# Layer two's front of the first tile and the sample, done in pieces inside layer one's last expert steps

## The chip, the cores and the metric

The kernel runs on one core of one Trainium2 chip. The metric is device microseconds of one execution. The kernel before takes 2525.78 us, the median of three runs (2523.29 to 2528.25).

## The reference, cut to what matters

One step of a two-layer encoder for 256 prompt tokens and 64 sample tokens, all in fp32. Each layer has a *mixer* half and a *PEER expert* half:

```python
h = rmsnorm(x, norm1_g);  z = h @ w_in          # xa, ga, xq, q, k, v, gates
ya = rg_lru(causal_conv(xa)) * gelu(ga)         # recurrence along the tokens
yb = pool_mixer(xq)                             # windows of 2, 4, 8, 16 tokens
yc = diff_attention(rotary(q), rotary(k), v)    # 8 heads, chunk-causal; the sample also sees its cache
x = x + (sum over branches of sigmoid(gate) * (branch @ proj)) @ w_out
h = rmsnorm(x, norm2_g);  top 16 of 16384 experts per head, 8 heads
x = x + sum(gelu(h . u[i]) * gate * v[i])       # u, v are gathered rows of 4 KB each
```

Tokens depend on each other only through the convolution, the recurrence, the pooling and the attention, and only on earlier tokens of the same stream. So the first 128 prompt tokens and the sample need nothing of the second 128 prompt tokens.

## The kernel before, in words

The 320 tokens lie in three tiles: tile 0 (prompt tokens 0 to 127), tile 1 (128 to 255, "tile two" in the texts) and tile 2 (the 64 sample tokens, held twice). Each engine has its own in-order program; they meet at counting semaphores only, so an instruction that waits holds up everything behind it on its engine.

A layer has three stages. The **front** normalises, turns h into HT, and makes the six feed-forward units of w_in (conv input, gelu gate, pooling input; `ff`, L1041 on PE), the convolution, the recurrence, the pooling, and then the eight attention heads (`head`: PE L919, ACT L1213, DVE L1475; rotary on POOL L678), ending with the heads' outputs turned into YT. In layer two its weights are loaded by SP from L527 on; the 21 parameter loads (L466) wait there for the end of layer one. The **merge** follows, and then the **expert stage**: 80 steps (`for s in range(GROUPS)`: PE L1143, ACT L1408, DVE L1856), 32 for tile 0, 16 for tile 2 and 32 for tile 1, in this order. POOL (`gathers`, L703) gathers four rows of 8 KB per token and step (1 MB each) into a ring of up to 12 buffers; a buffer is free again when PE has used it (`uv_free`). Two buffers join at picks 84 and 160 (`JOIN`, L81). The queries and the merge of tiles 1 and 2 run inside the earlier steps; in steps 41 to 72 DVE routes one of four parts of a coming unit per step (`ROUTES`, L145).

One step is a loop through three engines. DVE makes four dot products (`dots`, L1614), ACT their gelu (`weights`, L1239), DVE the routing part and then the weighing (`weigh`, L1623), ACT four diagonal matrices, and PE the matmuls that add the four rows (`experts`, L1001):

```python
                    dots(l, t, s)                    # DVE, L1861
                    ...
                        route(l, unit, [part])       # L1889
                    if s > 0:
                        weigh(l, t, g, s)            # L1891
```

On PE, tile 0's and tile 2's turns of layer two stand in step 78 (L1171), and the first feed-forward unit of their columns behind the last step (L1174).

Of the kernel before, what the change touches and what calls it, by code (L numbers as in the profile page):

```python
# [80 lines left out]
JOIN = [0] * 10 + [84, 160]  # L81
SLOT_OF, PREV, NTH = [], [], []
for _p in range(PICKS):
    _last = [max([q for q in range(_p) if SLOT_OF[q] == r], default=r - len(JOIN)) if JOIN[r] <= _p else PICKS
             for r in range(len(JOIN))]
    _r = _last.index(min(_last))
    PREV.append(max(_last[_r], -1))
    NTH.append(SLOT_OF.count(_r))
    SLOT_OF.append(_r)
RING_USES = [SLOT_OF.count(r) for r in range(len(JOIN))]  # L90
# [13 lines left out]
FF_SLOT = (0, 2, 3, 4, 1, 0)  # L104
# [29 lines left out]

def route_step(unit, part):
# [12 lines left out]
class Signal:  # L148


    def __init__(self, sem, per_layer, unit=1, start=0):
        self.sem, self.per_layer, self.unit, self.start = sem, per_layer, unit, start

    def at(self, l, n):

        return self.sem, (l * self.per_layer + n) * self.unit + self.start


def build(nc, x_prompt, x_sample, cache_v, state_conv, state_lru, state_pool,
# [3 lines left out]
          rot_table, pool_inv, layer_consts, peer_uv, gains, merge_w, out_w, query_w,  # L163
# [4 lines left out]
    with ctx:  # L168
# [45 lines left out]
        SALL12 = cut(2, 2 * PH, NK, at=0)  # L214
        SHIFT = cut(D_MODEL)
        W = sb("W", [P, SLOTS, KC, UNIT])
        W2 = [W[:, i].rearrange("p c n -> p (c n)").rearrange("p (k c n) -> p k c n", k=2, c=KC) for i in range(SLOTS)]
# [4 lines left out]
        SALL0 = cut(2 * PH, NK, at=0)  # L222
        HN0 = cut(D_MODEL)
# [28 lines left out]
        ZS = cut(2, 3 * HW)  # L252
        SUMS = [(S1, S2)[c % 2][:, c, :] for c in range(RC)]

        POOL_PARTS = ((POOL_HIST, SEQ, 0), (XQ_S + POOL_HIST, DEC_SEQ, SEQ))
# [30 lines left out]
        LCON = sb("LCON", [P, 3])  # L286
# [7 lines left out]
        PINV = sb("PINV", [P, 4, TOK])  # L294
# [48 lines left out]
        w_in_slot = [landing(f"w_in_slot{i}", SLOT_USES[i]) for i in range(SLOTS)]  # L343
        w_used = [signal(f"w_used{i}", SLOT_USES[i], start=1) for i in range(SLOTS)]
        qkv_in = [landing(f"qkv_in{i}", HEADS // 2) for i in range(2)]
        cache_in = [landing(f"cache_in{i}", 2 * HEADS // 2) for i in range(2)]
# [12 lines left out]
        ff_ps = signal("ff_ps", 6)  # L359
        ff_ev = signal("ff_ev", 12)  # L360
        xc_ready = signal("xc_ready", 1)
        bd_ps = signal("bd_ps", 2 * RC)
        sig_ev = signal("sig_ev", 2 * RC)
        decay = signal("decay", 1)
        oma = signal("oma", 1)
        root = signal("root", 1)
        ya_ready = signal("ya_ready", 1)
        d_ready = signal("d_ready", 1)
        pl_ps = signal("pl_ps", RC)
        pl_ev = signal("pl_ev", RC)  # L370
# [56 lines left out]
        uv_in = [landing(f"uv_in{i}", RING_USES[i]) for i in range(len(JOIN))]  # L427
# [38 lines left out]
        def small_loads(l):  # L466

            def row(name, n=1):
                return rows[ROW[name]:ROW[name] + n, :]
# [5 lines left out]
            def blocks(w, half):  # L475
# [12 lines left out]
                (SKR[:, :, :], peer_subkeys[l].rearrange("a k d -> k a d")),  # L488
# [19 lines left out]
        def _(sp):  # L508
# [18 lines left out]
            for l in range(DEPTH):  # L527
# [10 lines left out]
                for dst, src in loads:  # L538
                    sp.dma_start(dst, src).then_inc(small_in.sem, 16)
# [918 lines left out]
        def _(dve):  # L1458
# [242 lines left out]
            for t in SEQ_T:  # L1701
                normed(0, 0, t)
# [260 lines left out]
```

## Time and profile before

| | |
|---|---|
| time, median of three | 2525.78 us |
| the profiled execution's own time | 2523.54 us |
| its span, first to last instruction | 2521.6 us |
| mean granted TensorE clock | 0.883 |
| busy: PE, DVE, POOL, ACT | 75%, 63%, 31%, 27% |
| moved by DMA | 852 MB, mean 338 GB/s |

The span is 1.9 us shorter than the time of the same execution. Busy shares are means over stages with different limits, so the rows further down are read by stage. An fp32 matmul shows as two records. "Idle before" in square brackets is how long the engine had stood still, and what released it.

### The profile page before, as it was taken

Reading aid. Unit: us, or ns where it says so; the run is one execution under the profiler, and the core shown is the slowest. Engines: PE = TensorE matmul, PEld = TensorE weight load, DVE = VectorE, ACT = ScalarE, POOL = GpSimd, SP = SyncE. Lnnn points to the kernel's source line nnn. Section 1 sums busy time; section 2 is a strip of 40 time slices with the busy share of each in tenths; the row PEclk is TensorE's granted clock in tenths of the full one; section 3 lists DMA queues with packets and bytes.
Section 4 is the critical chain, followed back from the end, with each engine's and each line's share of the span. In section 5 each row is a group of like instructions: output and inputs, shape, how many; then the busy total and the mean of one; then the engine's idle time right before and its main releaser. Section 6 shows DMA issues by size and latency. Waiting matters only on the chain.

```text
span 2521.6 us, 31152 instructions
## 1 busy us (share of the span) xinstructions
PE 1898.0 (75%) x10740; PEld 1077.2 (43%) x10740; DVE 1588.6 (63%) x4318; ACT 677.9 (27%) x1691; POOL 780.1 (31%) x831
## 2 busy tenths in 40 slices
PE   7999988887777645555589999888777866555554
PEld 6556876654333211111165568765543432111111
DVE  3544165566788878777536431665666888777764
ACT  2423033332223222212233221333322332222121
POOL 0121022333333444344202210233334324344432
PEclk9999999999888877787899999999988887688777
DMA  6134849999999999999742357699999999999996
GB/s 217 65 130 166 316 199 417 417 412 419 419 413 369 418 421 400 421 421 421 326 155 78 126 205 270 275 417 417 404 419 420 415 370 410 403 411 421 421 421 271
DMA packets 156764, 852.11 MB, mean 338 GB/s; under 512 B 19312, under 2 KB 39280, under 8 KB 72640
## 3 DMA queue, kind: packets, MB, share of 16 engines
q0 software_dynamic: 95280, 677.24, 65.0%
q1 hardware_dynamic: 61328, 172.89, 18.7%
q8 instruction: 86, 1.41, 0.2%
q14 instruction: 70, 0.57, 0.1%
HBM read 843.35 MB, written 6.71 MB: 337 GB/s over the span
## 4 chain that ended last, share of the span: by engine, by line
DMA 30%; PE 23%; DVE 14%; issue 9%; PEld 8%; PEldq 5%; POOL 5%; DVEq 3%; ACT 2%; SPq 0%; ACTq 0%; POOLq 0%
DMA MIX_RINGS<-in_peer_uv_dram,IDX 15%; DMA WQKV_E<-in_peer_uv_dram,IDX 10%; PE ps L775 7%; PEldq L1019 5%; PEld ps L843 4%; DMA W<-in_peer_uv_dram,IDX 4%; PE ps L1049 3%; POOL MIX_RINGS L724 3%; PE ps L793 3%; DVE MIX_RINGS L1620 3%; DVEq L1464 3%; POOL W L724 2%; PE ps L781 2%; DVE W L1620 1%; PE ps L803 1%
## 5 line engine op out<-in xcount | busy, mean ns | idle before, releaser
L1017 PE MATMUL ps<-MIX_RINGS,GC 64*64 64x512 f32 x3200 | 662.0, 750 | 211.3 <-ACT GC L1248 200.0
L724 POOL DMA_INDIRECT MIX_RINGS<-in_peer_uv_dram,IDX x400 | 433.4, 1084 | 765.5 <-PEq L1019 442.0
L1017 PE MATMUL ps<-W,GC 64*64 64x512 f32 x1456 | 418.3, 776 | 297.4 <-ACT GC L1248 292.2
L1017 PEld LDWEIGHTS ps<-MIX_RINGS,GC 64*64 64x64 f32 x3200 | 158.3, 161 | 519.4 <-issue 288.5
L724 POOL DMA_INDIRECT W<-in_peer_uv_dram,IDX x182 | 196.0, 1077 | 439.5 <-PEq L1019 379.0
L1620 DVE CUSTOM_DVE_ANT_0 MIX_RINGS<-MIX_RINGS 128x1024 f32<-128x1024 f32 x224 | 269.0, 1223 | 83.3 <-DMA MIX_RINGS<-in_peer_uv_dram,IDX 78.9
L1017 PEld LDWEIGHTS ps<-W,GC 64*64 64x64 f32 x1456 | 97.7, 167 | 517.7 <-ACT GC L1248 295.7
L1248 ACT ACTIVATE GC<-twins,WV 128x64 f32<-128x64 f32 x640 | 170.3, 336 | 527.1 <-DVEq L1633 526.8
L1620 DVE CUSTOM_DVE_ANT_0 MIX_RINGS<-MIX_RINGS,WQKV_E 128x1024 f32<-128x1024 f32 x176 | 212.6, 1224 | 151.7 <-DMA MIX_RINGS<-in_peer_uv_dram,IDX 145.6
L1242 ACT ACTIVATE GV<-AV 128x4 f32<-128x4 f32 x160 | 32.9, 205 | 723.8 <-DVEq L1621 723.5
L1620 DVE CUSTOM_DVE_ANT_0 W<-W,MIX_RINGS 128x1024 f32<-128x1024 f32 x126 | 153.9, 1224 | 59.6 <-DMA W<-in_peer_uv_dram,IDX 52.2
L843 PE MATMUL ps<-HT,W 128*128 128x192 f32 x768 | 145.2, 351 | 44.0 <-issue 34.7
L775 PE MATMUL ps<-WQKV_E,HT 128*128 128x384 f32 x512 | 171.5, 489 | 0.0
L843 PEld LDWEIGHTS ps<-HT,W 128*128 128x128 f32 x768 | 138.0, 207 | 51.2 <-issue 51.1
L671 POOL TENSOR_TENSOR rot_a<-MIX_RINGS,ROTT 128x128 f32<-128x128 f32 (+1 forms) x48 | 19.9, 432 | 374.6 <-ACT MIX_RINGS L1210 374.6
L1017 PE MATMUL ps<-WQKV_E,GC 64*64 64x512 f32 x464 | 125.2, 662 | 2.2 <-ACT GC L1248 1.1
L775 PEld LDWEIGHTS ps<-WQKV_E,HT 128*128 128x128 f32 x512 | 95.0, 190 | 61.2
L906 PE MATMUL ps<-HT,W 128*128 128x256 f32 x512 | 114.3, 381 | 4.3 <-issue 4.3
L906 PEld LDWEIGHTS ps<-HT,W 128*128 128x128 f32 x512 | 96.0, 190 | 30.4 <-issue 18.0
L1620 DVE CUSTOM_DVE_ANT_0 W<-W,WQKV_E 128x1024 f32<-128x1024 f32 x56 | 68.5, 1226 | 49.7 <-DMA W<-in_peer_uv_dram,IDX 48.0
L724 POOL DMA_INDIRECT WQKV_E<-in_peer_uv_dram,IDX x58 | 64.1, 1105 | 107.2 <-PEq L1019 92.5
L1242 ACT ACT_TABLE_LOAD x72 | 92.4, 1283 | 1.3
(276 smaller groups left out, 2784.0 us busy)
## 6 DMA issues: line engine op xcount, KB each, us to landing
W<-in_merge_w_dram SPq DMA_DIRECT2D x40, 1024.0 KB, 5.0
W<-in_merge_w_dram SPq DMA_DIRECT2D x60, 512.0 KB, 14.1
WQKV_E<-in_qkv_w_dram SPq DMA_DIRECT2D x16, 1536.0 KB, 7.1
W<-in_query_w_dram SPq DMA_DIRECT2D x16, 1024.0 KB, 11.4
W<-in_w_in_dram SPq DMA_DIRECT2D x12, 1024.0 KB, 11.5
W<-in_query_w_dram SPq DMA_DIRECT2D x20, 512.0 KB, 11.4
W<-in_out_w_dram SPq DMA_DIRECT2D x8, 1024.0 KB, 13.9
MIX_RINGS<-in_peer_uv_dram,IDX POOLq DMA_INDIRECT x400, 14.6
```

The costliest lines, as they stand in the source:

```text
L724: pool.indirect_dma_start(UV[r], None, table, bass.IndirectOffsetOnAxis(IDX[:, n % DEEP, j:j + 1], 0))\
L775: i = pe.matmul(bank(n % 2, 0, 3 * HW), HT[:, c, COLS[t]], WQKV[par][:, c, :], start=c == 0, stop=c == KC - 1)
L793: i = pe.matmul(two(bank(b, 0, UNIT)), HT[:, c, 0:P], W2[b][:, :, c, :], start=c == 0, stop=c == KC - 1)
L843: m = pe.matmul(to, w[:, r, :], moving[:, r, P:TOK], start=n == 0, stop=n == len(rows) - 1)
L906: i = pe.matmul(bank(4 + 2 * slot, k * UNIT, (k + 1) * UNIT), W2[slot][:, k, c, :], HT[:, c, P:TOKD], start=c == 0, stop=c == KC - 1)
L1017: pe.matmul(ps[o:o + CHUNK, n:n + 512], w[r, :], v[r, d * 512:(d + 1) * 512], start=False, stop=False, skip_group_check=True)
L1019: pe.drain().then_inc(uv_free.sem, 2)
L1049: i = pe.matmul(bank(4 + n % 2, 0, TOK), W[:, FF_SLOT[u], c, k * P:(k + 1) * P], HT[:, c, 0:TOK], start=c == 0, stop=c == KC - 1)
L1242: act.activation(GV[:, :], AV[:, :], ACT.Gelu).then_inc(gv_ready.sem, 1)
L1248: act.activation(DG[:, p % N_DG, :], twins[:, 0:CHUNK], ACT.Copy, scale=WV[:, j:j + 1])\
L1464: dve.drain()
L1620: dve.tensor_tensor_reduce(u, u, HN[t], 1.0, 0.0, ALU.mult, ALU.add, AV[:, j:j + 1])
```

## The change

Layer two's front is split. For tile 0 and the sample (192 columns) it becomes 59 pieces, r = 0 to 58, two to each of the steps 50 to 79 of layer one (`A_SLOT` = 100). Piece 2s - 100 stands before the step's experts on PE, between gelu and diagonals on ACT, and behind the dots on DVE; piece 2s - 99 stands behind the experts on PE, behind the diagonals on ACT and behind `weigh` on DVE. Pieces 0 to 2 turn the tiles and the parameters, 3 to 14 are twelve feed-forward blocks of 128 columns, 7 to 10 the pooling, 15 to 22 the convolution and recurrence. Head h has pieces k = r - 19 - 4h: k = 0 and 1 the two halves of its qkv product, (2) the rotary on POOL, 3 the turns of q and k, 4 scores and maxima, exponentials, 5 probabilities, 6 their turns, 7 the value product and the output's squares; so k = 4 of one head shares a slot with k = 0 of the next, 5 with 1, 6 with 2, 7 with 3. Pieces 55 to 58 normalise the outputs and turn them. On DVE pieces k = 3 and 7 wait for PE's transposes and value product, and k = 5 for ACT's exponentials.

SP loads the parameters, a second, block-wise copy of the feed-forward columns (`early_w`, 512 KB a block), the qkv weights in halves of 768 KB and the caches for it, at the end of layer one's queue. POOL does head h's rotary and four stores ahead of gather 248 + 8h. The scratch for it lies in weight slots, so layer one's ring has eleven buffers from pick 84 to 180 and ten after it. The front behind layer one does tile 1 alone (128 columns): conv, pooling and recurrence start from kept states, and tile 0's keys and values are loaded back from the outputs. Also: the pooling's table of reciprocals becomes a small table of ratios, the score blocks of tiles 1 and 2 are copied by two instructions, and all three gate products stand behind the last head.

```diff
+RING = 12
+STAYS = (((0, PICKS),) * 10 + ((84, 180), (PICKS, PICKS)), ((0, PICKS),) * 10 + ((84, PICKS), (160, PICKS)))
...
+A_SLOT = 100
+A_HEADS = 19
+A_PACE = 4
...
+A_ROTARY = [4 * ((A_SLOT + A_HEADS + A_PACE * _h + 1) // 2) + 8 for _h in range(HEADS)]
...
+                    sp.wait_ge(*sso_ready.at(EARLY, 1))
+                    for u in range(3):
+                        ff_unit(u)
...
+                            sp.dma_start(KV0[:, par, 0, :], k_prompt[l, 0, 0:P, h].rearrange("p m d -> p (m d)"))\
+                                .then_inc(cache_in[par].sem, 16)
...
+                    parameters(1)
+                    for j in range(3 * RC):
+                        if j < 2:
+                            sp.wait_ge(*uv_free.at(0, 1 + max(p for p in range(PICKS) if SLOT_OF[0][p] == 10)))
+                        else:
+                            sp.wait_ge(*ff_ps.at(EARLY, j - 1))
+                        sp.dma_start(A_F[j % 2].rearrange("p c n -> p (c n)"), early_w[0, j])\
+                            .then_inc(w_in_slot[3 + j % 2].sem, 16)
...
+                            sp.wait_ge(*z_ps.at(EARLY, 3 * h + 1))
+                            early_half(h + 1, 0)
+                            sp.wait_ge(*z_ps.at(EARLY, 3 * h + 3))
+                            early_half(h + 1, 1)
...
+                pool.wait_ge(*z_ev.at(EARLY, 2 * h + 1))
+                rotate(EARLY, 2 * h, A_ZH[:, par:par + 1, :], ROTT[:, 0:1])
+                pool.wait_ge(*z_ev.at(EARLY, 2 * h + 2))
+                rotate(EARLY, 2 * h + 1, A_ZS[par].rearrange("p (t n) -> p t n", t=1), ROTT[0:DEC_SEQ, 2:3])
...
+                    if l == 0 and p in A_ROTARY:
+                        early_rotary(A_ROTARY.index(p))
...
+                    pe.wait_ge(*w_in_slot[3 + j % 2].at(0, SLOT_USES[3 + j % 2] + j // 2 + 1))
+                    if j >= 2:
+                        pe.wait_ge(*ff_ev.at(EARLY, j - 1))
+                    for c in range(KC):
+                        i = pe.matmul(bank(j % 2)[:, A_COLS], A_F[j % 2][:, c, :], HT[:, c, A_COLS],
+                                      start=c == 0, stop=c == KC - 1)
+                    i.then_inc(ff_ps.sem, 1)
...
+                for h in reversed(range(HEADS)):
+                    early_head(h, r - A_HEADS - A_PACE * h)
...
+                if k in (0, 1):
+                    pe.wait_ge(*qkv_in[k].at(EARLY, h + 1))
...
+                    w = (A_W0, A_W1)[k]
+                    for to, cols in ((bank(0, 0, 3 * HW), COLS[0]), (bank(1, 0, 3 * HW)[0:DEC_SEQ], COLS[2])):
+                        for c in range(KC // 2):
+                            i = pe.matmul(to, HT[:, k * KC // 2 + c, cols], w[:, c, :], start=k == 0 and c == 0,
+                                          stop=k == 1 and c == KC // 2 - 1, skip_group_check=True)
...
+                if k == 4:
+                    pe.wait_ge(*qt_ev.at(EARLY, h + 1))
+                    pe.wait_ge(*kt_ev.at(EARLY, h + 1))
+                    for m in range(2):
+                        pe.matmul(bank(2 + m, 0, P), A_QT[d[m], 0:P], A_KT[d[m], 0:P], start=True, stop=True,
+                                  skip_group_check=True).then_inc(s_ps.sem, 1)
...
+                if k == 6:
+                    pe.wait_ge(*p_ready.at(EARLY, 2 * h + 1))
+                    pe.transpose(bank(3, 0, P), A_PC[0], ident[:, :]).then_inc(pta_ps.sem, 1)
+                    pe.wait_ge(*p_ready.at(EARLY, 2 * h + 2))
+                    for c in range(3):
+                        i = pe.transpose(bank(2, c * CHUNK, (c + 1) * CHUNK),
+                                         A_PC[2][0:DEC_SEQ, c * P:(c + 1) * P], ident[0:DEC_SEQ, 0:DEC_SEQ])
+                    i.then_inc(ptb_ps.sem, 1)
...
+            def late_head(h):
+
+                g, par = divmod(h, 2)
+                z = ZH[par][:, 1, :]
+                pe.wait_ge(*rot_done.at(LATE_F, 2 * h + 2))
+                pe.wait_ge(*ex_done.at(LATE_F, 2 * h))
+                pe.transpose(bank(2, 0, P), z[:, 0:HW], ident[:, :]).then_inc(qt_ps.sem, 1)
+                pe.wait_ge(*pta_ev.at(LATE_F, h))
+                pe.wait_ge(*cache_in[par].at(LATE_F, 2 * g + 2))
+                pe.transpose(bank(3, 0, P), KV0[:, par, 0, :], ident[:, :])
+                pe.transpose(bank(3, P, 2 * P), z[:, HW:2 * HW], ident[:, :]).then_inc(kt_ps.sem, 1)
+                if h + 1 < HEADS:
+                    late_qkv(h + 1, range(KC // 2))
...
+                for m in range(2):
+                    d = slice(m * HD, (m + 1) * HD)
+                    pe.matmul(scores(1, m), QT[d, 0:P], KT[d, 0:2 * P], start=True, stop=True,
+                              skip_group_check=True).then_inc(s_ps.sem, 1)
+                if h + 1 < HEADS:
+                    late_qkv(h + 1, range(KC // 2, KC))
...
+                    if l == 0 and 2 * s >= A_SLOT:
+                        early(2 * s - A_SLOT)
                     experts(l, s)
+                    if l == 0 and 2 * s >= A_SLOT:
+                        early(2 * s + 1 - A_SLOT)
...
                 act.activation(GV[:, :], AV[:, :], ACT.Gelu).then_inc(gv_ready.sem, 1)
+                if l == 0 and 2 * s >= A_SLOT:
+                    early(2 * s - A_SLOT)
                 act.wait_ge(*wv_ready.at(l, s + 1))
...
+                if l == 0 and 2 * s >= A_SLOT:
+                    early(2 * s + 1 - A_SLOT)
...
+            def early_head(h, k):
...
+                if k == 4:
+                    dve.wait_ge(*s_ps.at(EARLY, 4 * h + 4))
...
+                if k == 6:
+                    dve.wait_ge(*ptb_ps.at(EARLY, h + 1))
+                    dve.tensor_copy(A_PTB, bank(2, 0, 3 * CHUNK)).then_inc(ptb_ev.sem, 1)
...
+                    if l == 0 and 2 * s >= A_SLOT:
+                        early(l, 2 * s - A_SLOT)
...
                     if s > 0:
                         weigh(l, t, g, s)
+                    if l == 0 and 2 * s >= A_SLOT:
+                        early(l, 2 * s + 1 - A_SLOT)
```

## Rows read from the trace of the kernel before

**Rows 1.** The page, the span in 40 slices: PE's and the DMA engines' line.

```profile
PE   7999988887777645555589999888777866555554
...
DMA  6134849999999999999742357699999999999996
```

**Rows 2.** Windows: late expert steps of layer one; layer two's front in three parts.

```profile
core 0: us, PE busy (x) PEld busy (x) DVE busy (x) ACT busy (x) POOL busy (x), PEclk, DMA share, GB/s
...
1062.00:1252.40 190.40, 106.64 (x624) 27.01 (x624) 126.14 (x303) 37.48 (x115) 77.61 (x69) 0.79 0.98 408
...
1257.40:1346.50 89.10, 80.33 (x346) 55.65 (x347) 44.86 (x85) 31.95 (x67) 5.59 (x11) 0.98 0.36 122
1346.50:1484.60 138.10, 133.66 (x649) 79.90 (x649) 67.34 (x253) 40.53 (x131) 35.11 (x76) 0.99 0.40 138
1484.60:1497.10 12.50, 11.76 (x57) 8.72 (x56) 5.53 (x8) 6.86 (x13) 0.00 (x0) 0.98 0.57 205
```

**Rows 3.** Timeline of ACT: the gelu of steps 49 and 79 of layer one.

```profile
954.67 0.21 ACT L1242 ACTIVATE GV<-AV 128x4 f32<-128x4 f32 x1 [0.84 <-DVEq L1621]
...
1252.16 0.20 ACT L1242 ACTIVATE GV<-AV 128x4 f32<-128x4 f32 x1
```

**Rows 4.** Timeline, layer two's front: the last experts, single pieces, the gates (start, length).

```profile
1256.67 0.60 PE L1017 MATMUL ps<-WQKV_E,GC 64*64 64x512 f32 x2
...
1266.36 3.81 PE L1029 MATMUL ps<-HT,W 128*128 128x128 f32 x32 [0.83 <-ACT HT L1200]
...
1324.85 8.23 DVE L1783 RECIPROCAL MIX_RINGS<-MIX_RINGS 128x1292 f32<-128x1292 f32 x1
...
1478.42 3.11 POOL L735 DMA_DIRECT2D out_dram<-SOT  x6 [5.20 <-DMA out_dram<-MIX_RINGS]
...
1484.56 7.17 PE L793 MATMUL ps<-W,HT 128*128 128x256 f32 x32
```

**Rows 5.** Timeline, layer two's heads: the links of one head.

```profile
1420.43 2.75 PE L775 MATMUL ps<-WQKV_E,HT 128*128 128x384 f32 x8
...
1423.11 0.93 PE L953 MATMUL ps<-MIX_RINGS 64*128 64x128 f32 x8
...
1426.01 0.47 ACT L1222 ACTIVATE MIX_RINGS<-ps,nb 128x256 f32<-128x256 f32 x1 [0.45 <-DVE nb L1493]
...
1428.04 0.17 DVE L1500 RECIPROCAL rec<-sme 128x2 f32<-128x2 f32 x1
...
1429.38 0.16 DVE L1500 RECIPROCAL rec<-sme 64x2 f32<-64x2 f32 x1
...
1433.36 0.36 DVE L1516 COPY MIX_RINGS<-ps 128x192 f32<-128x192 f32 x1 [2.68 <-PE ps L983]
```

**Rows 6.** Timeline of DVE, step 50 of layer one: first dot, routing, weighing.

```profile
957.21 1.23 DVE L1620 CUSTOM_DVE_ANT_0 MIX_RINGS<-MIX_RINGS 128x1024 f32<-128x1024 f32 x1 [0.16 <-issue]
...
962.00 0.49 DVE L1549 MAX8 MX<-WQKV_E 128x8 f32<-128x128 f32 x2
...
964.20 0.16 DVE L1628 TENSOR_TENSOR WV<-GV,GATE 128x4 f32<-128x4 f32 x1
```

**Rows 7.** Timeline, steps 68 and 69: routing, weighing and the expert matmuls behind it.

```profile
1141.98 0.17 DVE L1577 TENSOR_SCALAR CI<-BC 128x16 uint32<-128x16 uint32 x1
...
1145.83 0.16 DVE L1628 TENSOR_TENSOR WV<-GV,GATE 128x4 f32<-128x4 f32 x1
...
1150.51 1.12 PE L1017 MATMUL ps<-W,GC 64*64 64x512 f32 x2
...
1152.53 0.59 PE L1017 MATMUL ps<-W,GC 64*64 64x512 f32 x2
...
1154.07 0.16 DVE L1628 TENSOR_TENSOR WV<-GV,GATE 128x4 f32<-128x4 f32 x1
...
1156.29 2.65 PE L1017 MATMUL ps<-MIX_RINGS,GC 64*64 64x512 f32 x18
```

**Rows 8.** The page, DMA issues: 512 KB loads of merge_w on SP's queue (KB, us to landing).

```profile
W<-in_merge_w_dram SPq DMA_DIRECT2D x60, 512.0 KB, 14.1
```

More of the change, by code:

```diff
@@ L151, in __init__ @@
     def __init__(self, sem, per_layer, unit=1, start=0):
-        self.sem, self.per_layer, self.unit, self.start = sem, per_layer, unit, start
+        self.sem, self.unit, self.start = sem, unit, start
+        self.before = [sum(per_layer[:i]) for i in range(len(per_layer) + 1)] if isinstance(per_layer, tuple)\
+            else [i * per_layer for i in range(DEPTH + 2)]
     def at(self, l, n):
-        return self.sem, (l * self.per_layer + n) * self.unit + self.start
+        return self.sem, (self.before[l] + n) * self.unit + self.start
 def build(nc, x_prompt, x_sample, cache_v, state_conv, state_lru, state_pool,
@@ new lines, in late_qkv @@
+            def late_qkv(h, cs):
+                par = h % 2
+                if cs[0] == 0:
+                    pe.wait_ge(*qkv_in[par].at(LATE_F, h // 2 + 1))
+                    if h >= 2:
+                        pe.wait_ge(*z_ev.at(LATE_F, h - 1))
+                for c in cs:
+                    i = pe.matmul(bank(par, 0, 3 * HW), HT[:, c, COLS[1]], WQKV[par][:, c, :],
+                                  start=c == 0, stop=c == KC - 1)
+                if cs[-1] == KC - 1:
+                    i.then_inc(z_ps.sem, 1)
@@ new lines, in ff @@
+                        act.drain().then_inc(ff_ev.sem, 1)
+                for u in range(5):
+                    ff(u)
+                for c in range(RC):
+                    for j, (dst, row) in enumerate(((RG, "lru_ba"), (IG, "lru_bx"))):
+                        act.wait_ge(*bd_ps.at(LATE_F, 2 * c + j + 1))
+                        act.activation(dst[:, c, 0:P], bank(6 + j, 0, P), ACT.Sigmoid,
+                                       bias=PT[:, c, ROW[row]:ROW[row] + 1]).then_inc(sig_ev.sem, 1)
@@ new lines, in late_front @@
+                for h in range(HEADS):
+                    late_head(h)
+                act.wait_ge(*sso_ready.at(LATE_F, 1))
+                act.activation(rso[:, 1, :], sso[:, 1, :], ACT.Sqrt, bias=eps_c[:, :], scale=1.0 / HW)\
+                    .then_inc(sso_root.sem, 1)
+                gates(l, 0)
+                for hh in range(HEADS):
+                    act.wait_ge(*yt_ps.at(LATE_F, hh + 1))
+                    act.activation(YT[:, 2 * RC + hh, B_COLS], bank(6 + hh % 2, 0, P), ACT.Copy, scale=SUBG[:, 0:1])\
+                        .then_inc(yt_ev.sem, 1)
@@ L1325, in _ @@
                         .then_inc(yt_ev.sem, 1)
+            squares(SEQ_T)
+            turned(0, 0, SEQ_T)
+            for l in range(DEPTH):
+                if l == 0:
+                    joint_front()
+                else:
+                    late_front(l)
                 for u in range(GB):
                     if u + 1 < GB:
-                        gates(u + 1)
+                        gates(l, u + 1)
                     act.wait_ge(*mta_ps.at(l, u + 1))
@@ L1943 @@
     proj_ab = _np.concatenate([inputs["proj_a"], inputs["proj_b"]], axis=1)
+    order = [2 * RC + i for i in range(RC)] + [RC + i for i in range(RC)] + list(range(RC))
+    rows["early_w"] = blocks(inputs["w_in"][1:2, :, 0:COL_Q])[:, order]
     rows["gains"] = _np.concatenate([*(inputs[n][l:l + 1] for l in range(DEPTH) for n in ("norm1_g", "norm2_g")),
```

930 lines of the change are left out of this document (760 added, 170 removed).

## The prediction

> **What bounds the kernel now.** I read the page's slices first, then the windows by stage, then the timeline inside a stage. In the slices [rows 1] the pattern runs twice, once per layer: a front in which PE is mostly at 8 or 9 and DMA mostly at 1 to 5, then a long expert stretch in which DMA is at 9 and PE falls to 5. The windows put numbers on layer two's front and on layer one's last steps [rows 2]. In the late expert steps the DMA engines are at 0.98 and 408 GB/s, PE, on paper, 56% busy, DVE 66%. In the front behind, PE is 90% busy before the heads, 97% in them and 94% in the tail, with DMA at 0.36 to 0.57. So the front, 89.1 + 138.1 + 12.5 = 239.7 us, belongs to PE, the expert steps belong to the gathers. From the first to the second gelu of [rows 3] there are 30 steps in 297.5 us: 9.92 us each, four gathers of 1.05 MB at 422 GB/s.
>
> **The front behind: what it gives back.** It keeps 128 of 320 columns.
> Before the heads: tile two's HT is ready 9.0 us after the last expert matmul, as now (1257.3 to 1266.4 [rows 4]). Thirty-two 128-column matmuls (one unit; every fp32 matmul shows as two) take 3.81 us there, so five units take 19.1, ending at 28; the parameters are loaded beforehand, so the wait before the 320-column units goes. Then the gates' products and sigmoids (5), eight activations with a table load (4), 1 - a with its reciprocal (8.23 us for 1292 elements [rows 4], so 3.3 for 512, with two passes beside it 4.7), root, products and scans (3.3), the gelu product and the state's way through PE and DVE (3.3): 48.6 in place of 89.1, **-40.5**.
> Heads: now 17.3 each. For one tile the chain is: three transposes and half a qkv product (0.6 + 2.75 + 0.55 to start the scores) 3.9; scores to the maximum's scaling 2.1 (2.9 from 1423.11 to 1426.01, less tile one's 0.8 between); two exponentials 1.05; normalised difference 1.35 (1428.04 to 1429.38); transposes, copy, value product 1.9 (estimated as two thirds of what three tiles take): 10.3 [rows 5]. Eight, the last without a qkv half: 80.2, **-57.9**. The other qkv half (2.75) and POOL's rotary lie beside the chain. SP's key and value reloads and the 1.5 MB weights are issued a head or more ahead, POOL's store waits are bounded below.
> Tail: all three gate products now stand behind the last head (48 matmuls; 32 took 7.17 [rows 4], so 10.8), then eight small transposes and copies: 14.5, **+2**. Sum **-96**; between -78 (12 us a head, weights 5 us late) and -107 (9 us a head).
>
> **The expert steps: what it costs.** DVE runs its queue in order. One step without the pieces is, on DVE: four dots 4.8 (957.21 to 962.00 [rows 6]), one routing part (2.2 in this step [rows 6], 3.85 for the index part [rows 7]; I take 2.7 as the mean of the four), the weighing 0.3: 7.8, under the 9.9 of the gathers. What the change adds there, by rows: one head's maxima 2.1, probabilities 2.7 (twice 1.35), the KT copy and the output's copy and squares 2.0, a PTB copy 0.4, so 7.2 for two steps, which alone would still fit (22.8 us of DVE work against 25 of transfers with the new bytes).
> But the odd pieces stand right behind weigh(s) on DVE and right behind experts(s) on PE, and experts(s) itself waits for weigh(s). For k=4 (scores) and k=6 (probabilities turned) DVE asks for what PE issues in that same odd slot. So DVE stands idle while ACT builds the diagonals and PE runs the whole expert group, with the next step's dots queued behind the wait though their rows have landed. From weighing to the last expert matmul is 7.3 us in one step and 4.9 in the next [rows 7]; I take 6.3, since PE begins each burst after a pause, as in the first of them, where matmuls show 1.12 and then 0.59 us. In the k=4 slot PE also does the next head's first half *before* the scores (heads run in reverse): 16 recorded matmuls of 384 columns, twice the eight that took 2.75 us [rows 5], 5.4; scores with the cache 1.8.
> Step with k=4: 4.8 + 2.0 + 2.7 + 0.3 + 6.3 + 5.4 + 1.8 + 2.1 = 25.4. Step with k=6: 4.8 + 2.7 + 2.7 + 0.3 + 6.3 + 1.4 + 0.4 = 18.6. Eight pairs at 44.0 are 352, less 5.4 (no ninth head) and 10.8 (routing ends at step 72, four steps): 336 where 16 steps took 158.9, **+177**.
> Steps 50 to 60: the first waits for PE with the parameters, 17; step 51, 10. The twelve feed-forward blocks need 512 KB each, two a step, and each load waits for the block two before it; now such loads take 14.1 us to land in a busy stretch [rows 8]. By bytes alone a step would take (4.19 + 1.05) MB / 422 GB/s = 12.4, by landing plus some 2.9 us of matmuls (three quarters of the 3.81 of [rows 4], since a block has half the matmuls at 1.5 times the columns) 17: I take 14 for six steps, 84, nearer to the bytes since slower steps thin the gathers out. Then 12 (two taps), 12, and 19.4 (reciprocal 5.0 of 792 elements, scans). Sum 154 where 11 took 109: **+45**. Steps 77 to 79 finish the normalising: **-2**.
> Priced at nothing: ACT's pieces (3.2 us of exponentials with a table load hide behind the dots; uncovered, 3 a head); POOL's eight rotations and 32 stores ahead of the gathers (some 7 us each, behind a step pair of 44 with the ring full; in 10 us steps they would empty it); SP's 65 further loads, of which the halves are issued two steps ahead (layer two's own first loads come behind them, with all of the last steps to land); two smaller ACT copies for one per score block; the smaller pool table; ten ring slots in place of twelve from step 45 (ten sufficed for full DMA in the early slices, at most +10).
> Sum: 177 + 45 - 2 - 96 = **+124**. The profiled execution took 2523.54 us for a span of 2521.6, and the median of three is 2525.78, 2.2 above; 2523.5 + 124 gives 2647, and I say **2645**.
>
> **Rivals.** *The transfers stay the bound, and the change wins.* DMA at 0.98 in the late steps with idle PE speaks for it [rows 2]: a step then costs only its bytes, 6.3 + 12.6 + 2.1 + 0.8 = 21.8 MB at 422 GB/s, +52, net -44: **2479**. It needs the two waits of a head, 21 us together in my sum, to be under some 2 us; the net is zero at 21 - 124/8 = 5.5. Against it: the program's order, and [rows 5], where DVE's copy waits for PE in just this manner. The Trainium skill (Perfetto Trace Analysis, Identifying the Most-Contended Engine, and its Optimization Strategy) says to judge a regime by its busiest resource and to interleave regimes with different ones. By that rule this rival holds and the time is 2479. The row of this stretch agrees about which resource is busiest, but the rule does not price an in-order queue that waits in between.
> *PE stays at its lower level.* The clock granted in late steps is 0.79 [rows 2]; if the pieces run at 1.2 GHz, each head costs 1.0 more per wait, 5.4 more for the half and 1.8 for the scores, 8 x 9.2 = 74, less 5 for the last half: **2715**.
> *The front shrinks less.* POOL's wait for each store's landing (5.20 us [rows 4]) with the rotation and two issues makes about 8 us a head, under 10.3; were it 12.5, +18: **2663**.
>
> **How the numbers follow.** Forecast 0.62 (2590 to 2690), lower clock 0.18, smaller front 0.08, transfers the bound 0.12, of which 0.02 ends near no change. The measurement tells 0.2%, 5 us. Range **2575 to 2725**: the wait at 4.9 in place of 6.3 takes off 22, the larger front gain 11, blocks at 12.4 a step 10; upwards the clock's 70 and the front's 18 are not wanted both. Faster 0.10, same 0.02, slower 0.88.
>
> **What would show it.** Layer one's steps 61 to 76 alternate between about 25 and 18 us between gelus; the list of waits has DVE waiting for PE some 150 us in that stretch; DMA there falls to 0.6; the front behind is near 143 us. Steps near 12 us with DMA at 0.95 and no such wait would make it wrong, as would a front over 165.

## The result and the profile after

The changed kernel takes 2635.17 us (median of four runs, 2631.11 to 2638.07) where the kernel before takes 2525.77 in the same runs: ratio **1.0432**, 95% interval 1.0412 to 1.0451, 109 us slower. The forecast was 2645. The profiled execution took 2632.88 us for a span of 2631.0, so the sum below, 2632.88 - 2523.54 = 109.3, is made between two single executions.

The page's 40 slices, PE's and the DMA engines' line, to be held against [rows 1] (a slice is 65.8 us now):

```profile
PE   7999988886777548665665778988886777555555
...
DMA  6135769999999999876666547499999999999996
```

Two things have moved. In the DMA line the front between the layers was four slices (4, 2, 3, 5) and is now some two (from within the 5 to within the 7). And ahead of it the row of nines ends in 8, 7, 6, 6, 6, 6: the expert steps that carry the pieces no longer run at the speed of the transfers.

The windows by stage; the first is steps 50 to 60, the second 61 to 76, the other three the front behind (ahead of the heads, heads, tail). Columns as in [rows 2]:

```profile
core 0: us, PE busy (x) PEld busy (x) DVE busy (x) ACT busy (x) POOL busy (x), PEclk, DMA share, GB/s
969.40:1115.80 146.40, 105.16 (x646) 56.43 (x638) 104.07 (x278) 49.29 (x126) 52.54 (x55) 0.89 0.92 371
1115.80:1444.20 328.40, 200.13 (x956) 76.51 (x956) 152.34 (x454) 73.17 (x203) 101.81 (x153) 0.78 0.69 257
1472.50:1523.10 50.60, 36.31 (x248) 32.66 (x245) 23.38 (x47) 20.48 (x44) 2.85 (x6) 0.86 0.47 169
1523.10:1595.50 72.40, 56.63 (x216) 31.82 (x217) 26.33 (x101) 19.16 (x57) 17.53 (x46) 0.95 0.58 209
1595.50:1610.50 15.00, 13.66 (x58) 10.90 (x56) 2.30 (x5) 5.41 (x14) 1.27 (x3) 0.92 0.64 208
```

In the second row the DMA engines are at 0.69 and 257 GB/s, PE is busy 200 of 328 us, DVE 152: no engine is full. They wait for each other in turn, as the list of waits below shows.

The gelu of steps 70, 71 and 72 (timeline of ACT; steps 49 and 79 of before are in [rows 3]):

```profile
1312.71 0.21 ACT L1610 ACTIVATE GV<-AV 128x4 f32<-128x4 f32 x1 [1.50 <-DVEq L2144]
...
1329.70 0.20 ACT L1610 ACTIVATE GV<-AV 128x4 f32<-128x4 f32 x1 [5.05 <-DVEq L2144]
...
1354.61 0.20 ACT L1610 ACTIVATE GV<-AV 128x4 f32<-128x4 f32 x1 [2.08 <-DVEq L2144]
```

From step 70 to 71 it is 17.0 us, from 71 to 72 24.9, where each took 9.9 before: steps alternate, as they must when one has k = 6 and the next k = 4 behind its expert group. As a ledger by the gelus of the same steps (of step 50 at 962.17 before and 969.44 after, of 61 at 1070.44 and 1115.84, of 77 at 1232.34 and 1444.15, of 79 at 1252.16 and 1463.30), with the forecast beside it:

| stretch | before | after | change | forecast |
|---|---|---|---|---|
| up to the gelu of step 50 | 962.2 | 969.4 | +7.3 | 0 (ring: at most 10) |
| steps 50 to 60 | 108.3 | 146.4 | +38.1 | +45 |
| steps 61 to 76 | 161.9 | 328.3 | +166.4 | +177 |
| steps 77, 78 | 19.8 | 19.2 | -0.7 | -2 |
| the front behind, and what follows | | | -101.8 (109.3 less the four above) | -96 |

What the alternation is made of stands in the list of DVE's waits, steps 61 to 76 (total us, times, longest):

```profile
DVE ps L2488 <- PE ps L1275: 103.3, 8, 14.0
DVE W L2509 <- PE ps L1283: 57.9, 8, 8.2
```

161.2 us in sixteen waits, eight for the scores and eight for the turned probabilities, and next to nothing else. The same in the timeline, steps 70 and 71 (weighing is L2151, the expert matmuls L1158, a qkv half L1248):

```profile
1317.69 0.16 DVE L2151 TENSOR_TENSOR WV<-GV,GATE 128x4 f32<-128x4 f32 x1
...
1324.27 0.40 PE L1283 MATMUL ps<-ident,W 64*128 64x64 f32 x3
...
1324.70 0.36 DVE L2509 COPY W<-ps 128x192 f32<-128x192 f32 x1 [6.85 <-PE ps L1283]
1324.98 1.22 DVE L2143 CUSTOM_DVE_ANT_0 MIX_RINGS<-MIX_RINGS 128x1024 f32<-128x1024 f32 x1
...
1333.72 0.16 DVE L2151 TENSOR_TENSOR WV<-GV,GATE 128x4 f32<-128x4 f32 x1
...
1340.59 5.54 PE L1248 MATMUL ps<-YT_SALL,HT 128*128 128x384 f32 x16 [0.26 <-issue]
...
1347.18 5.57 PE L1248 MATMUL ps<-W,HT 128*128 128x384 f32 x16
...
1347.37 0.19 DVE L2488 MEMSET ps<- 64x64 f32 x2 [13.48 <-PE ps L1275]
```

DVE weighs at 1317.69, then stands still for 6.85 us until PE has done the whole expert group and four transposes (the last three are the line shown), and only then begins the dot at 1324.98, whose row had landed (POOL sent its last gather ahead of this stretch at 1298.21, the next at 1318.97). It weighs again at 1333.72 and stands still for 13.48 us: expert group, next head's half (5.54), scores. The other half, at 1347.18 ahead of the next expert group, costs nothing: DVE's maxima, dots, probabilities and routing lie beside it.

One head of the front behind, on PE:

```profile
1533.55 0.27 PE L1321 MATMUL ps<-ident,MIX_RINGS 128*128 128x128 f32 x1
...
1533.87 2.75 PE L1310 MATMUL ps<-WQKV_E,HT 128*128 128x384 f32 x8
1536.55 0.70 PE L1333 MATMUL ps<-MIX_RINGS 64*128 64x256 f32 x4
...
1541.04 0.44 PE L1339 MATMUL ps<-ident,MIX_RINGS 128*128 128x128 f32 x2 [1.01 <-DVEq L2540]
...
1542.50 0.27 PE L1321 MATMUL ps<-ident,MIX_RINGS 128*128 128x128 f32 x1
```

A head takes 8.95 us (1533.55 to 1542.50).

### The profile page after: what moved, and what is told of

The parts are those of the page before. It is cut to its first block, busy times and chain, and to the rows that moved or that the text cites. A ratio compares the mean times of both kernels' runs of the same rounds, so it can differ in the third digit from the quotient of the medians.

```text
span 2631.0 us, 31937 instructions
## 1 busy us (share of the span) xinstructions
PE 1945.1 (74%) x10932; PEld 1107.3 (42%) x10932; DVE 1591.6 (60%) x4381; ACT 716.3 (27%) x1784; POOL 787.9 (30%) x895
## 4 chain that ended last, share of the span: by engine, by line
DMA 24%; PE 20%; DVE 20%; issue 13%; PEld 6%; PEldq 4%; DVEq 4%; POOL 4%; ACT 3%; ACTq 0%; POOLq 0%; SPq 0%
DMA MIX_RINGS<-in_peer_uv_dram,IDX 17%; DVE MIX_RINGS L2143 5%; PEldq L1160 4%; PEld ps L984 4%; DMA WQKV_E<-in_peer_uv_dram,IDX 3%; PE ps L934 3%; DVEq L1987 3%; PE ps L916 3%; POOL MIX_RINGS L862 3%; PE ps L1158 3%; DMA W<-in_peer_uv_dram,IDX 3%; DVE W L2143 2%; PE ps L1408 2%; PEld ps L1047 1%; PE ps L944 1%
## 5 line engine op out<-in xcount | busy, mean ns | idle before, releaser
L1158 PE MATMUL ps<-MIX_RINGS,GC 64*64 64x512 f32 x3344 | 688.3, 746 | 322.4 <-ACT GC L1618 310.5
L862 POOL DMA_INDIRECT MIX_RINGS<-in_peer_uv_dram,IDX x418 | 446.4, 1068 | 903.6 <-PEq L1160 577.7
L1158 PE MATMUL ps<-W,GC 64*64 64x512 f32 x1296 | 369.1, 783 | 223.4 <-ACT GC L1618 218.8
L1158 PEld LDWEIGHTS ps<-MIX_RINGS,GC 64*64 64x64 f32 x3344 | 165.8, 161 | 658.7 <-ACT GC L1618 335.2
L2143 DVE CUSTOM_DVE_ANT_0 MIX_RINGS<-MIX_RINGS 128x1024 f32<-128x1024 f32 x242 | 289.2, 1222 | 63.5 <-DMA MIX_RINGS<-in_peer_uv_dram,IDX 57.0
L862 POOL DMA_INDIRECT W<-in_peer_uv_dram,IDX x162 | 171.8, 1060 | 365.4 <-PEq L1160 311.3
L1158 PEld LDWEIGHTS ps<-W,GC 64*64 64x64 f32 x1296 | 86.4, 169 | 399.7 <-ACT GC L1618 215.6
L984 PE MATMUL ps<-HT,W 128*128 128x192 f32 x768 | 146.6, 353 | 41.7 <-issue 25.6
L2143 DVE CUSTOM_DVE_ANT_0 W<-W,MIX_RINGS 128x1024 f32<-128x1024 f32 x106 | 128.9, 1224 | 35.8 <-DMA W<-in_peer_uv_dram,IDX 31.1
L1158 PE MATMUL ps<-WQKV_E,GC 64*64 64x512 f32 x480 | 139.1, 705 | 2.5 <-ACT GC L1618 1.2
L1610 ACT ACT_TABLE_LOAD x82 | 105.2, 1283 | 1.6
L779 POOL TENSOR_TENSOR rot_a<-MIX_RINGS,ROTT 128x64 f32<-128x64 f32 (+1 forms) x40 | 15.7, 410 | 289.3 <-ACT MIX_RINGS L1578 176.2
L984 PE MATMUL ps<-YT_SALL,W 128*128 128x192 f32 x512 | 88.5, 327 | 0.0
L934 PE MATMUL ps<-W,HT 128*128 128x256 f32 x384 | 87.3, 388 | 0.0
## 6 DMA issues: line engine op xcount, KB each, us to landing
MIX_RINGS<-in_peer_uv_dram,IDX POOLq DMA_INDIRECT x418, 12.8
```

Source lines behind the costliest of these rows:

```text
L862: pool.indirect_dma_start(UV[r], None, table, bass.IndirectOffsetOnAxis(IDX[:, n % DEEP, j:j + 1], 0))\
L934: i = pe.matmul(two(bank(b, 0, UNIT)), HT[:, c, 0:P], W2[b][:, :, c, :], start=c == 0, stop=c == KC - 1)
L984: m = pe.matmul(to, w[:, r, :], moving[:, r, P:TOK], start=n == 0, stop=n == len(rows) - 1)
L1158: pe.matmul(ps[o:o + CHUNK, n:n + 512], w[r, :], v[r, d * 512:(d + 1) * 512], start=False, stop=False, skip_group_check=True)
L1610: act.activation(GV[:, :], AV[:, :], ACT.Gelu).then_inc(gv_ready.sem, 1)
L2143: dve.tensor_tensor_reduce(u, u, HN[t], 1.0, 0.0, ALU.mult, ALU.add, AV[:, j:j + 1])
```

## The experiments

Each is an edit of the changed kernel unless it says otherwise. Times are medians, ratios are to the kernel before in the same runs.

**e1, the older head first on PE.** Does the next head's half, standing ahead of the scores, cost what it takes?

```diff
-                for h in reversed(range(HEADS)):      # PE
+                for h in range(HEADS):
                     early_head(h, r - A_HEADS - A_PACE * h)
```

> Edit: on TensorE the older head's piece stands first in a slot, so that the scores (k = 4) come ahead of the next head's first qkv half (k = 0) and no longer behind it. Nothing is added or taken away. Theory (VectorE's queue waits for whatever TensorE does between weighing and the scores): the wait in each of seven slots loses the half's 5.5 us, 38 us in all: 2597 us (2590 to 2607), and the list of waits has VectorE waiting for the scores some 65 us in place of 103. Rival (TensorE's whole work at its lower clock is the bound, 25 us busy in a pair of steps): the same work in another order, 2635. Rival (transfers, POOL's stores or SP's loads hold the gathers back): 2635.

2589.26 us, ratio 1.0251 (1.0233 to 1.0269): 46 less than the changed kernel where 38 were forecast, so just under the range. DVE's waits in the stretch:

```profile
DVE ps L2488 <- PE ps L1275: 65.9, 8, 8.9
DVE W L2509 <- PE ps L1283: 55.3, 8, 8.3
```

The wait for the scores fell from 103.3 to 65.9, the 38 of the forecast, and the other by 2.6; the sixteen steps take 40.9 us less. So it is PE's order, not its amount of work, that DVE pays for. Both rivals said no change.

**e2, the odd pieces behind the next dots on DVE.**

```diff
                     dots(l, t, s)
+                    if l == 0 and 2 * s - 1 - A_SLOT >= A_HEADS + 4:
+                        early(l, 2 * s - 1 - A_SLOT)
...
                         weigh(l, t, g, s)
-                    if l == 0 and 2 * s >= A_SLOT:
+                    if l == 0 and 0 < 2 * s + 1 - A_SLOT < A_HEADS + 4:
                         early(l, 2 * s + 1 - A_SLOT)
```

> Edit: on VectorE alone the odd pieces from r = 23 on stand behind the next step's dots in place of behind this step's weighing. Theory: both waits of a head then have the 4.8 us of dots beside them, so 16 steps lose about 4.2 us each (something is given back, since the exponentials and the value product now stand closer to their readers): -65, 2570 us (2555 to 2590). If only the wait for the scores mattered: about -35. Rivals (TensorE's whole work, or the transfers, are the bound): 2635.

2585.92 us, ratio 1.0239 (1.0219 to 1.0260): 49 less, inside the range but 16 short of its middle. The waits:

```profile
DVE ps L2488 <- PE ps L1275: 48.7, 7, 8.8
DVE MIX_RINGS L2143 <- DMA MIX_RINGS<-in_peer_uv_dram,IDX: 16.5, 11, 4.1
DVE W L2509 <- PE ps L1283: 14.5, 7, 2.6
```

98 us of the two waits went, the dots being beside them now, but part came back as new ones: for rows (16.5), and, further down that list, for the key transposes (8.2), the value product (7.0) and the exponentials (7.0), which now stand close to their readers. What follows: the cure on DVE's side is the weaker one.

**e3, the odd pieces ahead of the expert group on PE.** The direct test of the theory: DVE's order is left, and what it asks for is made before the expert group.

```diff
+                    if l == 0 and 2 * s + 1 - A_SLOT >= A_HEADS + 4:
+                        early(2 * s + 1 - A_SLOT)
                     experts(l, s)
-                    if l == 0 and 2 * s >= A_SLOT:
+                    if l == 0 and 0 < 2 * s + 1 - A_SLOT < A_HEADS + 4:
                         early(2 * s + 1 - A_SLOT)
...
                 if k == 6:
+                    pe.wait_ge(*ex_done.at(EARLY, 4 * h + 4))
                     pe.wait_ge(*p_ready.at(EARLY, 2 * h + 1))
```

> Edit: on TensorE alone the odd pieces from r = 23 on stand ahead of the step's expert group in place of behind it (and the turn of the probabilities also waits for the sample's exponentials). Theory: the scores and the turned probabilities are then ready when VectorE has weighed, both waits of a head go, and a pair of steps falls from 42 us to about 27, where TensorE (25 us of work) and the transfers (25) are the next bounds: 8 x 15 = 120 less, 2515 us (2500 to 2540); VectorE's waits for TensorE in the stretch fall from 161 us to under 40. Rival (the total of TensorE's work, its clock, or the transfers already bound it): 2635, within 15.

2535.14 us, ratio 1.0039 (1.0025 to 1.0054): 100 us less from the place of one call, inside the range and 20 above its middle. Sixteen steps take 228.3 us in place of 328.3:

```profile
DVE ps L2491 <- PE ps L1275: 26.7, 7, 6.4
DVE EXTRA L2485 <- PE ps L1262: 13.5, 6, 3.5
```

```profile
1121.70:1350.00 228.30, 180.85 (x948) 73.10 (x947) 154.78 (x454) 73.51 (x203) 110.75 (x152) 0.91 0.92 356
```

The first fence is DVE's two longest waits for PE there: the scores' wait fell from 103.3 to 26.7, that for the turned probabilities from 57.9 to 0.7, but the wait for the key transposes (`EXTRA`) is new. With two small ones 47 us of waits for PE are left (the expectation said under 40). The second fence is the window of the sixteen steps, DMA back from 0.69 to 0.92. A pair of steps takes 28.5 us, not 27.

**e4, the second half twice.** The rival with the second largest chance had PE's own work as the price. Here it is made larger where DVE does not wait for it.

```diff
-                            i = pe.matmul(to, HT[:, k * KC // 2 + c, cols], w[:, c, :], start=k == 0 and c == 0,
-                                          stop=k == 1 and c == KC // 2 - 1, skip_group_check=True)
+                            for again in range(1 + k):
+                                i = pe.matmul(to, HT[:, k * KC // 2 + c, cols], w[:, c, :], start=k == 0 and c == 0,
+                                              stop=k == 1 and c == KC // 2 - 1 and again == 1, skip_group_check=True)
```

> Edit: the second half of each early head's qkv product (k = 1, in an even slot ahead of the expert group) is added twice, 16 more recorded matmuls of 384 columns a head, 5.5 us, 44 us of TensorE work in all; q, k and v of these heads are therefore other numbers. Theory: this slot lies beside VectorE's maxima, dots, probabilities and routing, so the added work is hidden: 2635 to 2645 us. Rival (TensorE's whole work is the bound): 2679.

2633.73 us, ratio 1.0423 (1.0402 to 1.0444): no more than the changed kernel, though every head has this (one half above, ahead of the scores; the doubled one below):

```profile
1340.19 5.54 PE L1249 MATMUL ps<-YT_SALL,HT 128*128 128x384 f32 x16 [0.27 <-issue]
...
1346.78 10.73 PE L1249 MATMUL ps<-W,HT 128*128 128x384 f32 x32
```

10.73 us where there were 5.57, eight times, 41 us of PE work, hidden. With e1 the two sides are complete: half a qkv product is free in the even slot and costs all of its time in the odd one.

**e5, the ring alone,** put into the kernel before: `STAYS`, with ten buffers after pick 180, in place of `JOIN`.

```diff
-JOIN = [0] * 10 + [84, 160]
+STAYS = (((0, PICKS),) * 10 + ((84, 180), (PICKS, PICKS)), ((0, PICKS),) * 10 + ((84, PICKS), (160, PICKS)))
...
```

> Edit: the kernel before, with nothing but the changed kernel's ring in layer one (eleven buffers from pick 84 to 180, ten after it, in place of twelve from 160). In the changed kernel the gelu of step 50 already stands 7.3 us later than before, ahead of all pieces. Theory: that is the two buffers, so this kernel is 5 to 12 us slower than before: 2533 us, with the loss between steps 42 and 50 (full transfers have ten buffers under way in later steps too, so little comes after). Rival (the loss comes from something else that stands ahead of step 50): 2526, no change.

2532.69 us, ratio 1.0028 (1.0018 to 1.0039), so 7 us, within 5 to 12. Where they are lost this run does not settle: the execution that was profiled took 2526.39 us, the shortest of eight, 2.9 more than the profiled one of before. Its gelu of steps 40 and 50:

```profile
857.76 0.20 ACT L1246 ACTIVATE GV<-AV 128x4 f32<-128x4 f32 x1 [4.74 <-DVEq L1625]
...
962.91 0.21 ACT L1246 ACTIVATE GV<-AV 128x4 f32<-128x4 f32 x1 [2.05 <-DVEq L1625]
```

Steps 40 to 50 take 105.2 us, 2.9 more than before (859.92 to 962.17), and steps 50 to 79 another 4.6 (its gelu at 1257.54, before 1252.16); the rest of the execution gives some 4.6 back. So in this execution the loss is not all between steps 42 and 50, where the expectation put it. The changed kernel takes 9.1 more over the same steps. The windows of these, before and changed:

```profile
859.92:962.17 102.25, 51.52 (x328) 12.84 (x320) 84.14 (x221) 29.29 (x71) 45.62 (x42) 0.78 0.99 408
```

```profile
858.13:969.44 111.31, 59.20 (x320) 14.19 (x316) 86.89 (x224) 28.00 (x70) 40.93 (x41) 0.71 0.96 387
```

408 GB/s x 102.25 is 41.7 MB, 387 x 111.31 is 43.1: the first two feed-forward blocks and the parameters, 1.4 MB, already cross here, 3.3 us at 421 GB/s. By this estimate ring and bytes make 6 of the 9; the last 3 stay open, the single runs of this kernel lying up to 6 us either side of their median.

**e6, e3 and e1 together.**

> Edit: e3 (odd pieces from r = 23 on ahead of the expert group on TensorE) and e1 (the older head's piece first) together. In e3 VectorE still waits 26.7 us for the scores in seven slots, because the next head's first half stands ahead of them, and that half waits 6.2 us for VectorE's output copies. Theory: the scores then need only the key copy, both waits go, 20 to 30 us: 2510 us (2500 to 2522), faster than the kernel before. Rival (TensorE, 80% busy in that stretch of e3, is by now the bound, so the half only moves to a place as dear): 2535, within 5.

2530.41 us, ratio 1.0015 (1.0005 to 1.0024): 5 less than e3, not 25. The number is the rival's. Only the wait for the scores went (26.7 us in e3, 0.2 here). The one for the key transposes stayed (13.5, now 16.1), the one for the turned probabilities came back (0.7, now 12.8), and DVE's waits for rows doubled (12.1, now 24.4, over all their buffers). The three longest:

```profile
DVE MIX_RINGS L2146 <- DMA MIX_RINGS<-in_peer_uv_dram,IDX: 20.3, 13, 3.8
DVE EXTRA L2485 <- PE ps L1262: 16.1, 7, 3.7
DVE W L2512 <- PE ps L1284: 12.8, 5, 5.9
```

Steps 71 and 72, POOL's queue and one dot, and the window of the sixteen steps:

```profile
1267.59 0.94 POOL L862 DMA_INDIRECT MIX_RINGS<-in_peer_uv_dram,IDX  x1 [3.38 <-PEq L1160]
...
1268.83 1.87 POOL L862 DMA_INDIRECT MIX_RINGS<-in_peer_uv_dram,IDX  x1 [0.30 <-issue]
...
1272.58 1.23 DVE L2146 CUSTOM_DVE_ANT_0 MIX_RINGS<-MIX_RINGS 128x1024 f32<-128x1024 f32 x1 [2.67 <-DMA MIX_RINGS<-in_peer_uv_dram,IDX]
...
1274.54 0.64 POOL L779 TENSOR_TENSOR rot_a<-YT_SALL,ROTT 128x64 f32<-128x64 f32 x2 [3.84 <-ACT YT_SALL L1682]
...
1280.10 1.03 POOL L862 DMA_INDIRECT MIX_RINGS<-in_peer_uv_dram,IDX  x1 [0.30 <-issue]
```

```profile
1116.40:1339.10 222.70, 179.96 (x953) 73.76 (x953) 154.28 (x454) 73.61 (x202) 110.59 (x152) 0.92 0.92 366
```

PE had freed all four buffers of its group by 1269.4 (the qkv half follows it then), but after the second gather POOL stands in front of the rotary (1274.54, 3.84 us of waiting for the copied qkv), and the third gather goes out at 1280.10. A dot meanwhile waits 2.67 us for its row. PE is 81% busy in the window, DMA at 0.92, and neither reading tells which is at fault: e9 does.

**e7, the output copies behind the routing part on DVE,** added to e6 (the copies and squares of k = 7 are called behind `route`, ahead of `weigh`).

```diff
-            def early_head(h, k):
+            def early_head(h, k, late=False):
...
-                if k == 7:
+                if k == 7 and late:
...
                         route(l, unit, [part])
+                    if l == 0 and 2 * s >= A_SLOT:
+                        for h in range(HEADS):
+                            if 2 * s - A_SLOT - A_HEADS - A_PACE * h == 7:
+                                early_head(h, 7, True)
```

> Edit: e6, and on VectorE the output copies and squares (k = 7) behind the routing part in place of ahead of it. Theory: VectorE's 7 us of waits for the value products go, but the next head's first half waits for these copies, some 2 us later a head, ahead of the expert group: between -7 and +8 against e6. It tells whether VectorE's queue or TensorE's is the longer one in those steps by then: faster if VectorE's, slower if TensorE's.

2529.01 us, ratio 1.0013 (1.0004 to 1.0022): no difference from e6 that this can tell. Inconclusive: neither queue is shown to be the longer.

**e9, POOL's rotary two gathers later,** added to e6.

```diff
-A_ROTARY = [4 * ((A_SLOT + A_HEADS + A_PACE * _h + 1) // 2) + 8 for _h in range(HEADS)]
+A_ROTARY = [4 * ((A_SLOT + A_HEADS + A_PACE * _h + 1) // 2) + 10 for _h in range(HEADS)]
```

> Edit: e6, with POOL's rotary and stores of each early head two gathers later (ahead of gather 250 + 8h in place of 248 + 8h). In e6 POOL waits for the head's copied qkv while TensorE has already given two buffers back, so that these two gathers start some 9 us late and VectorE's dots wait 24 us for rows in that stretch (transfers at 0.91). Theory (POOL's queue is what e6 ran into): half to all of those waits go, 10 to 20 us: 2516 us (2508 to 2524). Rival (TensorE's total, 80% busy, is what e6 ran into): 2530, within 4.

2507.11 us, ratio 0.9927 (0.9910 to 0.9944): 23 less, a little more than the range. The sixteen steps:

```profile
1119.20:1321.40 202.20, 177.23 (x948) 73.54 (x948) 156.84 (x454) 74.06 (x203) 109.99 (x149) 0.94 0.98 391
```

```profile
DVE MIX_RINGS L2146 <- DMA MIX_RINGS<-in_peer_uv_dram,IDX: 3.8, 4, 1.5
```

The transfers are at 0.98, DVE's waits for rows fell from 24.4 to 5.0 us (the line and a small one), and PE's busy time hardly changed (177 us in place of 180). So POOL's order was what e6 ran into, and the rival that had hit e6's number had the wrong cause.

**e11, the same edit on the changed kernel alone.**

> Edit: the changed kernel with e9's edit alone (POOL's rotary and stores two gathers later). It was worth 23 us on top of e6. Theory (as long as VectorE waits 161 us for TensorE, the rows of the next steps have landed anyway, so POOL's order is covered): 2635 us, within 6. Rival (POOL's order is a loss of its own, whatever else waits): 2612.

2631.53 us, ratio 1.0416 (1.0398 to 1.0433), overlapping the changed kernel's interval. What is worth 23 us once DVE's waits are gone is covered while they stand.

**e8, all odd pieces from r = 3 on ahead of the expert group,** added to e6.

```diff
-                    if l == 0 and 2 * s + 1 - A_SLOT >= A_HEADS + 4:
+                    if l == 0 and 2 * s + 1 - A_SLOT >= 3:
                         early(2 * s + 1 - A_SLOT)
                     experts(l, s)
-                    if l == 0 and 0 < 2 * s + 1 - A_SLOT < A_HEADS + 4:
+                    if l == 0 and 0 < 2 * s + 1 - A_SLOT < 3:
                         early(2 * s + 1 - A_SLOT)
```

In the changed kernel ACT waits for pieces behind the expert group in steps 50 to 60 as DVE does later (list of ACT's waits):

```profile
ACT YT_SALL L1636 <- PE ps L1199: 19.2, 4, 7.2
ACT YT_SALL L1639 <- PE ps L1199: 18.3, 3, 9.4
ACT W L1639 <- PE ps L1199: 15.5, 3, 6.7
```

> Edit: e6, and the odd pieces from r = 3 on (feed-forward blocks, pooling, gates) stand ahead of the expert group on TensorE too. In e6 ScalarE waits some 58 us between steps 50 and 60 for pieces that stand behind the expert group, with the next gelu queued behind. Theory: these waits go, but the transfers are already at 0.95 there, so only the slack is won: 5 to 10 us, 2523 us (2517 to 2529). Rival (that stretch is bound by the blocks' loads alone): 2530, as e6.

2522.91 us, ratio 0.9998 (0.9988 to 1.0008), 7.5 less than e6, as forecast. Of the 7.5, 2.2 is the kernel before, which took 2526.10 us beside e6 and 2523.95 beside e8, and the two intervals overlap; so against e6 alone this gain is barely clear of noise. e10 below tests the edit again.

**e10, e8 and e9 together.**

> Edit: e8 and e9 together. Theory (each was a queue of its own): the sum of the two, 2509 us (2500 to 2520), under the kernel before by over 0.2%. Rival (the transfers' bytes already hold e6 in both stretches): 2530, as e6.

**2501.33 us**, ratio **0.9912** (0.9896 to 0.9929): 0.9% faster than the kernel before. It is 5.8 us under e9, with the same runs of before beside both, so e8's edit is worth some 6 us there too, and the two gains nearly add up (29 of 31 us). Steps 50 to 60 and 61 to 76:

```profile
967.10:1107.90 140.80, 103.93 (x634) 60.12 (x632) 104.81 (x278) 49.77 (x127) 54.38 (x59) 0.91 1.00 408
1107.90:1313.90 206.00, 178.66 (x949) 73.47 (x949) 156.17 (x454) 74.16 (x202) 105.42 (x146) 0.94 0.95 379
```

DMA is at 1.00 and 0.95 where the changed kernel had 0.92 and 0.69. The work is that of the changed kernel; only places in two queues, PE's and POOL's, differ.

## Why the prediction was right

**The bound.** The forecast gave the front to PE and the expert steps to the gathers, and said that putting one beside the other would leave both waiting. The second window above has just that: nothing in it is full.

**The steps with heads** (+177 forecast, +166.4 measured). The mechanism, DVE's in-order queue behind weighing, is shown three ways: the list of waits (161.2 us; "some 150" in the forecast, while its own terms make 8 x 13.5 - 5.4 + 8 x 7.7 = 164), e1 (the half taken out of the wait) and e3 (the two waits cut from 161.2 to 27.4 us, -100 of the 166). Of the 166, queue order makes at least 126, since e9 does the same work in 202.2 us. The other 40, with DMA at 0.98, are mostly the added bytes: 391 GB/s x 202.2 us is 79 MB, where 408 x 161.9 is 66, and 13 MB at 422 GB/s take an estimated 31 us. Term by term: the wait with k = 4 was put at 6.3 + 5.4 + 1.8 = 13.5 and shows 13.48 in step 71; that with k = 6 at 6.3 + 1.4 = 7.7 and shows 6.85 in step 70 (means of eight: 12.9 and 7.2). A pair of steps was put at 42.0 on the mean and takes 328.3 / 8 = 41.0.

**Steps 50 to 60** (+45, +38.1). The first step, waiting for the parameters, takes 14.8 (17 forecast); the next seven, with the blocks, 14.0, 14.1, 9.6, 12.8, 11.8, 14.0 and 9.8, so 86 (10 + 84): 12.3 on the mean, with DMA at 0.98, close to the bytes' 12.4 and not the 14 that was taken; the last three 45.5 (43.4). What the forecast did not see is that ACT waits ten times for a block, 53 us in the list under e8, with the next gelu queued behind. In e8 23 us of that are left (6.7, 13.6 and 3.1), yet the seven steps still take 84.9 (DMA at 0.99): the bytes held them, and these waits were covered. What e8 wins is in the last three steps, 40.4 in place of 45.5, whose odd pieces it moves ahead too.

**Priced at nothing.** The ring was not nothing: 7 us (e5), inside the "at most +10". POOL's rotations and stores were rightly called covered "behind a step pair of 44 with the ring full; in 10 us steps they would empty it": e11 shows the first half of that sentence, and e9 the second, in steps that took 13.9 us in e6.

**The front** (-96, -101.8). Ahead of the heads 50.6 us (forecast 48.6), heads 72.4 (80.2), tail 15.0 (14.5). The heads are the mis-sized term: 10.3 forecast, 8.95 measured. From scores to the turned probabilities it is 4.5 us (1536.55 to 1541.04), just the 2.1 + 1.05 + 1.35 of the forecast; but the transposes and the half before the scores take 3.0 in place of 3.9, since the key copy is hidden beside the half, and the end 1.5 in place of 1.9.

**The sum.** The total is nearer than its terms. Three rows of the ledger came out 6.9, 10.6 and 5.8 us under the forecast; 7.3 up to step 50, which the sum had at nothing, and 1.3 in steps 77 and 78 hide over a third of that, by luck. Of the 10.6, 3 lie in the kernel before: its steps 61 to 76 take 161.9, not the 158.9 that was taken off. And the lower end of the range, 2575, is not what its three terms make: 2645 - 22 - 11 - 10 = 2602.

**The rivals.** *PE at its lower level* fell: the halves take 5.54 us for 16 records, per record what [rows 5] shows, though the mean granted clock of the stretch is 0.78; and e4's added 41 us cost nothing. *The front shrinks less* fell (138.0 us). *The transfers stay the bound*, 2479, was wrong for this kernel, and what it needed, both waits of a head under some 2 us, is what e3 to e10 made: with each queue mended the time goes to 2535, 2530, 2507 and 2501. The Trainium skill's advice to interleave regimes with different bounds (Perfetto Trace Analysis, Optimization Strategy) is therefore borne out by e10 and not by the change itself. The Trainium skill also says that the queues of ScalarE, VectorE and GpSimd are strictly first in, first out (PSUM — Partial Sum Buffer, Engine vs sequencer instructions). This case's traces agree for all three: 13.48 us on DVE, 9.4 at the longest on ACT, 3.84 on POOL in e6, each with ready work behind the wait.

## What to carry to other kernels

Work that fits beside a loop by its busy time has still to be placed in every in-order queue of that loop: a piece that reads another engine's result belongs in a place where that result is already made, so write down, for each wait that is added, what stands ahead of it on the producer and what is queued behind it on the reader. Here the wait's price was the producer's whole queue since the loop's own handover, the expert group and a half it did not need. Mend the longest such wait first and read the profile again, since a queue that is covered (POOL's, worth 4 us or nothing in e11) is worth 23 us as soon as the one in front of it is gone.

## What the runs showed that was not expected

- The rival's number in e6 with another cause: PE 81% busy and no gain looked like PE as the bound, and two gathers moved ahead of one wait on POOL gave 23 us with PE's work unchanged.
- POOL's small rotary operations (64 x 32) took 1.11 and 1.22 us in e6 while DVE made dots, and 0.24 and 0.27 where it made none, and the dots beside them 1.26 to 1.38 in place of 1.22. No run was made to single this out:

```profile
1251.42 1.38 DVE L2146 CUSTOM_DVE_ANT_0 MIX_RINGS<-MIX_RINGS 128x1024 f32<-128x1024 f32 x1
...
1251.79 1.11 POOL L781 TENSOR_TENSOR W<-rot_a 64x32 f32<-64x32 f32 x1
...
1276.77 0.24 POOL L781 TENSOR_TENSOR W<-rot_a 64x32 f32<-64x32 f32 x1
```
